# S5 preparation spread over rows, sum of experts in quarter tiles of TensorE, routing up to six groups ahead

## The reference

```python
q = (xt @ wq).reshape(t, PEER_HEADS, 2, PEER_HALF)
sc = einsum('thpc,pkc->thpk', q, subkeys)
sv, si = top_k(sc, 16)                     # 16 best of 128 keys in each half
cand = sv[..., 0, :, None] + sv[..., 1, None, :]
cs, cpos = top_k(cand.reshape(t, PEER_HEADS, -1), 16)
idx = take_along_axis(cidx, cpos); gate = softmax(cs)
act = gelu(einsum('td,tkd->tk', xbb, u_tab[ib]))
y = einsum('tk,tkd->td', gb * act, v_tab[ib])
```

## Time and profile before

| what | value |
|---|---|
| median of 3 runs | 1592.37 us (1583.6 to 1593.71) |
| the profiled execution's own time | 1590.52 us |
| its span in the profile | 1588.4 us |
| PE busy | 1328.5 us, 84% of the span |
| DVE busy | 1101.5 us, 69% |
| ACT busy | 768.3 us, 48% |
| POOL busy | 591.3 us, 37% |
| moved by DMA | 603.11 MB, mean 380 GB/s |
| PE matmul of the experts (L903), mean of a record | 633 ns (1824 records of the eight ring buffers in `rings`) |

### The profile page before, as it was taken

How to read it: one execution, slowest core, us unless ns; L and a number is a source line. 1 busy time by engine, 2 the same in 40 slices (tenths; PEclk the granted TensorE clock), 3 DMA queues, 4 the chain that set the end, 5 groups by cost and what they waited for, 6 DMA issues and landing times.

```text
span 1588.4 us, 15028 instructions
## 1 busy us (share of the span) xinstructions
PE 1328.5 (84%) x3872; PEld 582.0 (37%) x3872; DVE 1101.5 (69%) x2525; ACT 768.3 (48%) x2120; POOL 591.3 (37%) x517
## 2 busy tenths in 40 slices
PE   8999789988596788788999777888999887878786
PEld 4544444433242333343444333333344432222222
DVE  2347865766665799998564599999675586666654
ACT  2324543544344666765333556667353354444443
POOL 0024333434143344453332344443342353444440
PEclk9999899999799998899999899898999999999999
DMA  9569999999799989999999989989999899999996
GB/s 358 187 242 408 401 378 417 416 417 417 282 413 416 372 347 371 372 415 383 376 415 411 374 340 385 381 352 415 379 408 411 343 399 421 421 421 422 420 422 259
DMA packets 105401, 603.11 MB, mean 380 GB/s; under 512 B 9314, under 2 KB 9442, under 8 KB 39780
## 3 DMA queue, kind: packets, MB, share of 16 engines
q0 software_dynamic: 73728, 536.90, 83.2%
q1 hardware_dynamic: 31588, 65.26, 11.0%
HBM read 601.08 MB, written 1.05 MB: 379 GB/s over the span
## 4 chain that ended last, share of the span: by engine, by line
PE 32%; DVE 31%; DMA 21%; ACT 7%; issue 3%; DVEq 3%; ACTq 1%; POOL 0%; SPq 0%; POOLq 0%
PE ps L903 16%; DMA rings<-in_uv_tab_dram,idx 15%; PE ps L699 12%; DVE rings L1293 12%; DMA wst<-in_wq_dram 4%; DVE mem L1200 2%; DMA mem<-in_s_b_dram 2%; PE ps L892 2%; DVE dgs L1293 2%; DVE mem L1211 1%; ACT dgs L649 1%; DVE mem L1182 1%; DVE mem L1209 1%; ACT L643 1%; ACT wgt L646 1%
## 5 line engine op out<-in xcount | busy, mean ns | idle before, releaser
L903 PE MATMUL ps<-rings,dgs 128*128 128x512 f32 x1824 | 899.4, 633 | 187.1 <-ACT dgs L649 186.9
L449 POOL DMA_INDIRECT rings<-in_uv_tab_dram,idx x456 | 527.2, 1156 | 829.0 <-PE ps L903 741.0
L1293 DVE CUSTOM_DVE_ANT_0 rings<-rings,h 128x1024 f32<-128x1024 f32 x456 | 547.9, 1222 | 144.1 <-DMA rings<-in_uv_tab_dram,idx 130.0
L903 PEld LDWEIGHTS ps<-rings,dgs 128*128 128x128 f32 x1824 | 345.9, 199 | 678.9 <-issue 347.5
L643 ACT ACTIVATE gel<-dots 128x1 f32<-128x1 f32 x512 | 101.6, 198 | 462.4 <-DVE dots L1293 455.5
L649 ACT ACTIVATE dgs<-cst,wgt 128x128 f32<-128x128 f32 x512 | 205.6, 402 | 37.0 <-issue 2.3
L646 ACT ACTIVATE wgt<-gel,share 128x1 f32<-128x1 f32 x512 | 150.8, 295 | 36.6 <-issue 1.8
L699 PE MATMUL ps<-wst,hT 128*128 128x512 f32 x320 | 151.4, 611 | 8.7 <-DMA wst<-in_wq_dram 8.7
L903 PE MATMUL ps<-dgs 128*128 128x512 f32 x224 | 115.8, 642 | 22.9 <-ACT dgs L649 22.9
L449 POOL DMA_INDIRECT dgs<-in_uv_tab_dram,idx x56 | 62.4, 1114 | 100.6 <-PE ps L903 95.5
L699 PEld LDWEIGHTS ps<-wst,hT 128*128 128x128 f32 x320 | 61.4, 195 | 86.5 <-issue 84.9
(11 more groups left out here) (190 smaller groups left out, 948.2 us busy)
## 6 DMA issues: line engine op xcount, KB each, us to landing
wst<-in_wq_dram SPq DMA_DIRECT2D x15, 2048.0 KB, 20.0
wst<-in_w_out_dram SPq DMA_DIRECT2D x4, 2048.0 KB, 19.7
wst<-in_glu_w_dram SPq DMA_DIRECT2D x4, 2048.0 KB, 29.7
rings<-in_uv_tab_dram,idx POOLq DMA_INDIRECT x456
rings<-in_w_in_dram SPq DMA_DIRECT2D x3, 2048.0 KB, 16.7
rings<-in_w_in_dram SPq DMA_DIRECT2D x2, 1024.0 KB, 7.4
dgs<-in_w_in_dram SPq DMA_DIRECT2D x1, 2048.0 KB, 19.4
...
```

The lines of the kernel that those rows point to most:

```text
L449: nc.gpsimd.indirect_dma_start(out=ring[g % RING], out_offset=None, in_=uv_tab, in_offset=bass.IndirectOffsetOnAxis(ap=idx[n % 4][:, s:s + ...
L903: ins = PE.matmul(ps[:, 4 + 2 * t + b, :], diag[:, g % DIAGS, :], ring[g % RING][:, D + b * BANK:D + (b + 1) * BANK], start=(g % (PH * TOP ...
L1293: V.tensor_tensor_reduce(out=u, in0=u, in1=h[:, t, :], scale=1.0, scalar=0.0, op0=ALU.mult, op1=ALU.add, accum_out=dots[n % 2][:, s:s + 1] ...
```

## The change

1. **Quarter tiles.** `expert` issues four matmuls of 64 x 64 x 512 in place of two of 128 x 128 x 512. The diagonal's two 64 x 64 blocks (token half 0 and 1) are used once for each half of the channels b; the output of token half `half` and channel half b goes to partitions 64 b to 64 b + 63 of bank 4 + 2t + half. `y_sum` reads them back with four DVE instructions of 64 partitions.
2. **Routing by a table.** ROUTE_AT names the row at which each group's routing begins; the six steps (the exponential is one now) keep their distances 0, 2, 4, 6, 6, 8. Groups 9 to 15 begin at rows 96 to 166, and groups 17 to 23 at 242 to 324. AHEAD = 16 buffers hold indices and gates.
3. **S5 preparation** in ten stages at rows 78 to 108: `s5_dt`, `s5_th`, `s5_dec`, `s5_n`, `s5_trig`, `s5_k`, `s5_b0`, `s5_b1`, `s5_bT`, `s5_bT_copy`. The load of `s5_b` stands behind `load_w(7)` alone.
4. **Rows.** The queries (1, 0), (1, 1), (1, 2) begin at rows 76, 84 and 92 (88, 105 and 117 before). S5 takes nine rows per chunk: it begins at the same rows 139 and 267, its last chunk 7 rows sooner, and GLU, norm and queries behind it too.

```diff
-ROUTE = {0: "route_keys", 2: "route_pairs", 4: "route_best", 6: "route_index", 8: "route_gate"}
-EXP_AT = 6
+AHEAD = 16
+ROUTE = (("route_keys", 0), ("route_pairs", 2), ("route_best", 4), ("route_exp", 6), ("route_index", 6),
+         ("route_gate", 8))
+ROUTE_AT = {1: 0, 2: 16, 3: 26, 4: 40, 5: 50, 6: 72, 7: 80, 8: 88, 9: 96, 10: 104, 11: 112, 12: 120, 13: 134, 14: 150,
+            15: 166, 16: 234, 17: 242, 18: 250, 19: 260, 20: 276, 21: 292, 22: 308, 23: 324, 24: 362, 25: 370, 26: 378,
...
-    at(5, 2, ("s5_angle",))
-    query(5, 8, 1, 0)
-    at(6, 2, ("s5_setup",))
-    query(6, 9, 1, 1)
-    query(7, 5, 1, 2)
+    for slot, *names in ((78, "s5_dt"), (79, "s5_th"), (80, "s5_dec"), (81, "s5_n"), (82, "s5_trig"), (84, "s5_k"),
+                         (86, "s5_b0"), (90, "s5_b1"), (106, "s5_bT"), (108, "s5_bT_copy")):
+        at(0, slot, (names[0],))
+    query(0, 76, 1, 0)
+    query(0, 84, 1, 1)
+    query(0, 92, 1, 2)
...
-            slot = 11 + 10 * c
-            at(g, slot - 1 if c == 0 else slot - 7, ("s5_in", t, c))
+            slot = 11 + 9 * c
+            at(g, slot - 1 if c == 0 else slot - 6, ("s5_in", t, c))
...
-            at(g, 89 + 2 * b, ("glu_mm", t, b, 0, 4))
+            at(g, 82 + 2 * b, ("glu_mm", t, b, 0, 4))
...
-        norm(g, 97, 5 + 2 * t)
+        norm(g, 90, 5 + 2 * t)
         for b in range(4):
-            query(g, 103 + 6 * b, 2 + t, b)
+            query(g, 96 + 6 * b, 2 + t, b)
...
+    for n, slot in ROUTE_AT.items():
+        for name, i in ROUTE:
+            at(0, slot + i, (name, n))
...
-            load_w(7, 8, 9, 10)
+            load_w(7)
             sp.wait_ge(mix_done, T)
             sp.dma_start(b_raw, s5_b).then_inc(ld_b, 16)
+            load_w(8, 9, 10)
...
-                for b in range(2):
-                    ins = PE.matmul(ps[:, 4 + 2 * t + b, :], diag[:, g % DIAGS, :],
-                                    ring[g % RING][:, D + b * BANK:D + (b + 1) * BANK],
+                for half, b in ((0, 0), (1, 1), (0, 1), (1, 0)):
+                    rows = slice(64 * half, 64 * half + 64)
+                    ins = PE.matmul(ps[64 * b:64 * b + 64, 4 + 2 * t + half, :], diag[rows, g % DIAGS, rows],
+                                    ring[g % RING][rows, D + b * BANK:D + (b + 1) * BANK],
                                     start=(g % (PH * TOPK) == 0), stop=(g % (PH * TOPK) == PH * TOPK - 1))
...
                 for b in range(2):
-                    residual(t, b, ps[:, 4 + 2 * t + b, :])
+                    for half in range(2):
+                        xs = x[64 * half:64 * half + 64, t, b * BANK:(b + 1) * BANK]
+                        ins = V.tensor_tensor(xs, xs, ps[64 * b:64 * b + 64, 4 + 2 * t + half, :], ALU.add)
+                    ins.then_inc(x_done, 1)
```

More of the change, by code:

```diff
@@ L276, in trunk @@
         row = sb("row", [P, 2, TOPK])
-        idx = [sb(f"idx{i}", [P, TOPK], U32) for i in range(4)]
-        cs, gexp, share, dots, gel, wgt = (
-            [sb(f"{n}{i}", [P, TOPK]) for i in range(2)] for n in ("cs", "gexp", "share", "dots", "gel", "wgt"))
+        idx = [sb(f"idx{i}", [P, TOPK], U32) for i in range(AHEAD)]
+        cs, gexp, dots, gel, wgt = (
+            [sb(f"{n}{i}", [P, TOPK]) for i in range(2)] for n in ("cs", "gexp", "dots", "gel", "wgt"))
+        share = [sb(f"share{i}", [P, TOPK]) for i in range(AHEAD)]
         s5p = sb("s5p", [P, 3 * S5_TILES])
@@ L665, in _ @@
                 run(WORK[n].get(s, []))
-                if s == EXP_AT and n + 1 < GROUPS:
-                    gate_exp(n + 1)
                 if s % PACE == PACE - 1:
@@ L1112, in s5_setup, with s5_k @@
                 V.scalar_tensor_tensor(kf, kf, ROUND, mag, ALU.subtract, ALU.subtract).then_inc(n_ok, 1)
+                dve.drain()
+            def s5_k():
                 dve.wait_ge(cs5_ok, 1)
@@ L1135, in s5_setup, with s5_scaled, s5_b0, s5_b1 @@
                 dve.drain()
-                dve.wait_ge(ld_b, 16)
-                for r in range(2):
-                    for dst, k_, r_ in ((bt1, kr, r), (bt2, ki, 1 - r)):
-                        V.tensor_tensor(dst.rearrange("p (i n) -> p i n", i=S5_TILES), bc(k_, [None, 16]),
-                                        b_raw[:, r_, :].rearrange("p (i n) -> p i n", i=S5_TILES), ALU.mult)
-                    dve.drain()
-                    for g in range(2):
-                        half = slice(64 * g, 64 * g + 64)
-                        ins = V.tensor_tensor(bs[half, :, r, :, g, :],
-                                              bt1[half, :].rearrange("p (c j n) -> p c j n", c=8, j=4),
-                                              bt2[half, :].rearrange("p (c j n) -> p c j n", c=8, j=4),
-                                              (ALU.subtract, ALU.add)[r])
-                    if r == 0:
-                        dve.drain()
-                ins.then_inc(b_ok, 1)
+            def s5_scaled(r):
+                for dst, k_, r_ in ((bt1, kr, r), (bt2, ki, 1 - r)):
+                    V.tensor_tensor(dst.rearrange("p (i n) -> p i n", i=S5_TILES), bc(k_, [None, 16]),
+                                    b_raw[:, r_, :].rearrange("p (i n) -> p i n", i=S5_TILES), ALU.mult)
+                dve.drain()
+                for g in range(2):
+                    half = slice(64 * g, 64 * g + 64)
+                    ins = V.tensor_tensor(bs[half, :, r, :, g, :],
+                                          bt1[half, :].rearrange("p (c j n) -> p c j n", c=8, j=4),
+                                          bt2[half, :].rearrange("p (c j n) -> p c j n", c=8, j=4),
+                                          (ALU.subtract, ALU.add)[r])
+                return ins
+            def s5_b0():
+                dve.wait_ge(ld_b, 16)
+                s5_scaled(0)
+                dve.drain()
+            def s5_b1():
+                s5_scaled(1).then_inc(b_ok, 1)
             def s5_frac(t, c):
@@ L1276, in route_index @@
                 dve.drain()
-                V.scalar_tensor_tensor(idx[n % 4][:, :], row[:, 0, :], float(NK), row[:, 1, :], ALU.mult,
+                V.scalar_tensor_tensor(idx[n % AHEAD][:, :], row[:, 0, :], float(NK), row[:, 1, :], ALU.mult,
                                        ALU.add).then_inc(idx_ok, 1)
@@ L1294, in dot_product @@
                                        accum_out=dots[n % 2][:, s:s + 1]).then_inc(dot_ok, 1)
-            stage = dict(norm_ms=norm_ms, norm_h=norm_h, hT_copy=hT_copy, z_out=z_out, s5_angle=s5_angle, qkT_copy=qkT_copy,
+            stage = dict(norm_ms=norm_ms, norm_h=norm_h, hT_copy=hT_copy, z_out=z_out, s5_th=s5_th, qkT_copy=qkT_copy,
                          att_max=att_max, att_den=att_den, sgu_var=sgu_var, sgu_norm=sgu_norm, sgu_gate=sgu_gate, mix=mix,
-                         mixT_copy=mixT_copy, w_sum=w_sum, q_copy=q_copy, y_sum=y_sum, s5_setup=s5_setup, s5_rot=s5_rot,
+                         mixT_copy=mixT_copy, w_sum=w_sum, q_copy=q_copy, y_sum=y_sum, s5_n=s5_n, s5_k=s5_k,
+                         s5_b0=s5_b0, s5_b1=s5_b1, s5_rot=s5_rot,
                          s5_frac=s5_frac, s5_add=s5_add, s5_scan=s5_scan, s5_back=s5_back, glu_sum=glu_sum, norm_r=norm_r)
-            router = dict(route_keys=route_keys, route_pairs=route_pairs, route_best=route_best, route_index=route_index,
+            stage |= dict(route_keys=route_keys, route_pairs=route_pairs, route_best=route_best, route_index=route_index,
                           route_gate=route_gate)
@@ L1308, in _ @@
             run(PRELUDE)
-            for name in ROUTE.values():
-                router[name](0)
             for g in range(GROUPS * TOPK):
@@ L1313, in _ @@
                 run(WORK[n].get(s, []))
-                if s in ROUTE and n + 1 < GROUPS:
-                    router[ROUTE[s]](n + 1)
                 dot_product(g)
```

41 lines of the change are left out of this document (23 added, 18 removed).

## The result

The changed kernel takes **1553.3 us**, the median of four runs (1552.16 to 1554.3), against 1592.33 of the kernel before beside it: ratio **0.977**, with a 95% interval of 0.974 to 0.980. Run again later, on the chip of the last group of experiments, it took 1554.36 (1551.43 to 1556.39) against 1588.4, again 0.977. The forecast of 1559 is 6 us above that. The profiled execution took 1553.37 us with a span of 1551.6, so the spans differ by 36.8 us.

A forecast was written before the change was run, and what follows sets the result against it. DMA's transfers at 422 GB/s were taken as the ceiling, with 98 us lost below it. Terms -12 - 13 + 0 + 3 - 6 - 5 + 1.5 gave -31.5 us, from 1590.52 to 1559 us; range 1534 to 1590.

The forecast's parts named there:

- S5 preparation, -12: 400 to 430 us: DVE's wait for s5_b and PE's for DVE's scaling both go, 12 of 13.0 us lost.
- First S5 phase, -13: S5 of tile 0: rows 139 to 210 take 182 us, with eight more rows 202 against 215.5, so -13 us.
- Second S5 phase, 0: S5 of tile 1: four routings instead of five, 217 us against 215, taken as 0, bounds +3 and -5.
- Crowding in rows 72 to 128, +3: Seven routings there fill DVE to 91%, so waits for queries' PE work count: +3 us, bounds 0 and +15.
- Quarter tiles, -11 and +1.5 for the sum: Four tiles side by side, 0.86 us per row, save 11 us in GLU and queries; y_sum's extra instructions cost 1.5.
- the GLU's -6: GLU stretches: quarter tiles win 6 of the 10.2 us lost there.
- The queries' -5: Query stretches: quarter tiles win 5 of 31 us, since much of those is not waiting.
- Residual, +0.5 at the end and +1 inside: y_sum: four instructions for two cost 1.4 us each time; net +0.5 at the end, +1 inside the kernel.
- A: Rival: shorter PE work lowers the clock, slowing stretches with streamed blocks; up to +88 us, middle 1610 us, chance 8%.
- B: Rival: row products' tiles run two at a time, 1572 us (8%), or in turn, over 2100 us (1%).
- C: Rival: crowding costs +15 us in rows 72 to 128 and tile 1's phase +3; 1574 us, chance 12%.
- D: Rival: earlier PE release of buffers also wins half of the second S5 phase's and queries' losses; 1534 us, chance 14%.

The follow-up runs named there:

- e4: The kernel before with S5 preparation spread over rows 78 to 108, the s5_b load moved forward, queries at rows 76, 84, 96: 1575.47 us, ratio 0.991.
- e10: The kernel before with only the load of s5_b moved behind the first of the four wq blocks: 1576.13 us, ratio 0.992.
- e1: The changed kernel with the product of a row at full width, two matmuls of 128 x 128 x 512: 1563.98 us, ratio 0.985.
- e8_again: The changed kernel with groups 14, 15 routed at rows 180, 212, 16 to 20 at 234 to 262, 21 to 23 at 290, 314, 344: 1535.15 us, 0.966.
- e7: The changed kernel with groups 14 and 15 routed from rows 180 and 212 instead of 150 and 166: 1546.09 us, ratio 0.9754.
- e9: The table of e8_again with group 13 at row 160, 14 at 184, 16 to 20 at 234 to 258, 21 at 288: 1532.58 us, ratio 0.964.
- e3: The changed kernel with S5 chunks ten rows apart again and what follows the phase moved back: 1559.93 us, ratio 0.982.
- e6: The changed kernel with groups 20 to 23 routed from rows 280, 300, 322, 344 instead of 276, 292, 308, 324: 1548.71 us, ratio 0.9765.
- e2: The kernel before with only the quarter tiles and the sum in four instructions: 1575.99 us, ratio 0.993.

## Why the prediction was right

The forecast was -31.5 us; measured were -39 in the first comparison and -34 in the last, where the kernel before was 4 us faster. The mechanism, transfers as the ceiling and time won only where they stood still, held. The terms one by one:

- **S5 preparation, -12: right.** -12.0 in e4, -12.3 in e10; the trace shows 12.3 for rows 96 to 104. The 3.5 behind them, rows 104 to 139, are more likely the table's, whose routings are done before: kernels with the new table lose 0.2 (e1) to 3.5 us there (e8_again; the changed kernel again: 3.1), those with the old rows 4.1 to 6.0. (The working has a slip that changes nothing: from 387.77 to 394.12 are 6.35 us, not 6.2.) The reason given, both waits, was too broad: e10 takes away the load's part only and has all of it.
- **First S5 phase, -13: too large.** Rows 139 to 211 took 187.0 us, not 182, and lost 17.2 us, only 2.9 less than before. The sum of DVE's work was not too small: DVE was busy 174.1 us of the 187.0, below the 182. (The sum adds durations that overlap: two scans of 1.21 us take 2.33 together.) What failed is the step from it to a time: it took work and DMA as if they could even out over 72 rows. In rows 139 to 180, with routings 13, 14 and 15, DVE is busy 111.48 of 117.3 us and the rate is 361 GB/s; in rows 180 to 211, with none, DVE has 7 us to spare, but DMA is at its ceiling of 421 and cannot catch up. A ring of nine rows carries no more than about 22 us (an estimate, nine rows of 2.48). Moving two routings made it 177.9 us (e7, one of them out of the phase) and 179.7 (e9, with nearly the same work). Each half has its own bound, and the slower in each counts.
- **Second S5 phase, 0: right** in place, 199.5 us against 198.9, with four routings and the end of one in it. Five in e3 made it 204.0, three in e6 191.4, two and half of one in e8_again 184.1.
- **Crowding in rows 72 to 128, +3: did not come.** In the changed kernel rows 72 to 96 lose 1.9 us and rows 104 to 128 0.3. At full width, in e1, the first of these lose 6.2 (e4, with the old table, 1.4): the crowding is there, and quarter tiles hide it. DVE's waits for the query product, the longest 12.7 us before, are at most 5.3 us with them.
- **Quarter tiles, -11 and +1.5 for the sum: a little too small, and in the wrong places.** e1 and e2 give -11 to -13 net. The GLU stretches do lose 7.7 us less than before, but e1 without the tiles has that too (1.0 and 3.1 us lost), so in the changed kernel the GLU's -6 was 0: the other parts had already taken it. The queries' -5 was about 10 (e1 against the changed kernel: 11.3 in rows 0 to 96 and 352 to 400, 1 the other way in the rest). I took "much of those is not waiting" from a DMA share near 1, but the share counts engines that are occupied, not bytes: rates of 397 at full width (e1, rows 352 to 384) became 414.
- **Residual, +0.5 at the end and +1 inside:** four instructions in 2.80 us where two took 1.28, +1.5. What follows the last row's start is longer by the same 1.5 in the changed kernel, but by 0.7 in e2, e3, e6 and e7, close to the forecast's 0.5. The difference is the clock of the last row's product. First the changed kernel, its last row and its sum, then the last row of e7:

```profile
1539.47 1.98 PE L920 MATMUL ps<-rings,dgs 64*64 64x512 f32 x8 [0.48 <-ACT dgs L667]
1541.53 2.80 DVE L1118 TENSOR_TENSOR x<-x,ps 64x512 f32<-64x512 f32 x4 [3.18 <-PE ps L920]
```

```profile
1529.99 1.09 PE L918 MATMUL ps<-rings,dgs 64*64 64x512 f32 x8 [0.79 <-ACT dgs L665]
```

The granted clock is 0.50 there in the changed kernel (1.2 GHz) and full in e7 (2.4 GHz). This 0.9 us is the one price of the lower clock that the traces show by itself.

By lost time and by stretch, whatever part of the change it is due to, the first phase gave 10 us less than forecast; the preparation and the rows behind it gave 4 more, the GLU 2, the query stretches and rows 0 to 96 together 9.5 (14.5 for 5), and 3 of crowding did not come. So part of the closeness of 1559 to 1553 is luck between terms.

Of the rivals, **A** (the clock falls, slower) had its condition and not its price, but for the 0.9 us at the end. The granted clock fell from 0.942 to 0.781 on the mean, and from 0.98 to 0.69 in the last stage. There the rows keep their 2.48 us, since 1.72 us of PE, or 1.98 with the drain, fits into that. In the query stretches the clock is 0.80 to 0.87 and the lost time is smaller than before, so the block at 1.2 GHz behind six rows at 1.2 GHz that A priced did not become the rule. The Trainium skill, TensorE: Matmul & The Clock Gate, The HAM clock gate, has activity release the full clock; the rows agree, 0.96 in the GLU where PE is busy 36.14 of 39.9 us. What the full clock throughout would have given in the query stretches no run here isolates.

**B** fell: 0.86 us per row is what four tiles side by side take; two at a time would be 1.72 and in turn 3.44 at full clock. **C** did not occur. **D** (PE more of the bound than I said) was partly true: in the query stretches, where the tiles gave about 10 us for 5, not in the second S5 phase, which lost 23.6 us before and 25.1 after.
